# Routing of a hybrid mixer and mixture-of-experts block: both levels of the choice at once, the first selection on VectorE, rows normalised in pieces, and the first gather among the up matmuls

## The chip, the cores and the metric

The kernel runs on one core of one Trainium2 chip. The metric is the device time of one launch in microseconds (us), as the median of three runs.

## The reference

One layer over x of 256 tokens by 2048 channels, in fp32. What matters here is its second half:

```python
def _hier_moe(h, w_rg, b_rg, w_re, b_re, w1, w3, w2):
    lg = (ht @ w_rg).astype(jnp.float32) + b_rg.astype(jnp.float32)
    pg = jax.nn.softmax(lg, axis=-1)
    p_top, g_idx = lax.top_k(pg, 1)
    le = jnp.einsum("td,dge->tge", ht, w_re).astype(jnp.float32) + b_re.astype(jnp.float32)
    le_sel = jnp.take_along_axis(le, ..., axis=1)[:, 0]
    l2, e_idx = lax.top_k(le_sel, TOPK_IN_GROUP)
    gate = jax.nn.softmax(l2, axis=-1) * p_top
    expert = g_idx * EXP_PER_GROUP + e_idx
    ...
        return (jax.nn.silu(xb @ w1[e]) * (xb @ w3[e])) @ w2[e]

x = x + (jax.nn.sigmoid(mix_a) * ya + jax.nn.sigmoid(mix_b) * yb) @ w_out
x = x + _hier_moe(_rmsnorm(x, norm_ffn), w_rg, b_rg, w_re, b_re, w1, w3, w2)
return _rmsnorm(x, norm_final)
```

There are 4 groups of 8 experts. Each token chooses one group and the two best experts in it. An expert has three weights of 4 MB each (2048 by 512), so all 32 have 402 MB. Ahead of this stand two mixers (a gated delta rule with 8 heads and gated linear attention with 4), whose projections take 120 chunks of weights of 1 MB.

## The kernel before

Each engine has one program, written out by hand in its order, and semaphores tie them together. The mixer stages and the output projection come first (until about 960 us). TensorE multiplies chunks of weights that ScalarE and VectorE have split into two parts (`chunk`, L1361 to L1363; L668; L931). While TensorE makes the last output columns, it also transposes x1 (L1644) and multiplies it with the router's weights (L1654), which gives the logits.

**Routing.** VectorE (L1222 to L1299) sums the squares, GpSimd makes the reciprocal root `rstd2` (L627, L628), and ScalarE scales x1 by it into `h2`, in two copies of 2048 columns, one for each half of the tokens (L871). VectorE adds the biases to the logits (L1246, L1247), finds the largest group, masks the experts to that group, and finds first and second in it. `link(...)` makes the next instruction wait until this one is finished. The result is `Mt`, the mask of tokens by 32 experts (L1273), and `Wt`, their weights (L1287). TensorE counts ranks over tokens with five products (L1682 to L1686). From them VectorE makes `pos`, the slot of a token in its expert (L1291), and the number of rounds of 64 tokens an expert needs (`rounds_ready`, L1299). Every engine reads that number into a register (`value_load`, in the program's order a TENSOR_LOAD). It is one round for these inputs.

**Experts.** Experts run in 16 pairs, with 64 token slots each. For each pair GpSimd compares `pos` with `iota` into the 0/1 matrix `sel` (L642, L646) and weights it into `selg` (L649). TensorE gathers the rows by a product of `h2` with `sel`, in four quarters (L1702), and VectorE multiplies each quarter by the norm's scale into `xeT` (L1308, semaphore `xe`). TensorE transposes `selg` (L1710), ScalarE copies it (L884). Then come the up matmuls for both experts, w1 and w3 in four quarters each (L1729), the activation (L889, L1315, L1318, transposed at L1738), the down matmuls (L1749), and the products that add the result into x1 (L1765, L1324). The gather of the next pair stands among the matmuls of the one before.

**Weights.** SyncE alone loads them (`load_pair`, L452), in transfers of 1 MB, into a ring of 16 slots, 24 to a pair. The first 16 go out as places come free from the stages before; the later ones wait for `slotM_free`, which each quarter of the up matmuls raises by two at its end, and each quarter of the down matmuls too.

## Time and profile before

| | |
|---|---|
| median of 3 runs | 1941.43 us (1941.38 to 1942.59) |
| the profiled execution | 1936.88 us |
| its span in the profile | 1935.1 us |
| mean granted TensorE clock | 0.977 |
| busy: TensorE, VectorE, ScalarE, GpSimd | 1796.2, 638.6, 431.1, 176.8 us |
| read from memory | 534.42 MB |

### The profile page before, as it was taken

The page shows a single profiled execution, that of the slowest core. Times are in us where ns is not written, and L with a number is a line of the kernel's source. Part 1 is how long each engine was busy: PE and PEld are TensorE (multiplying, and loading weights), DVE is VectorE, ACT ScalarE, POOL GpSimd, SP SyncE. Part 2 cuts the span into 40 slices and gives each one's busy share as a digit, 9 for nine tenths or more (in the row PEclk, how much of TensorE's full clock was granted, in tenths as well). Part 3 has the DMA queues.
Part 4 walks back from the last instruction along what each step waited for, and adds up shares of the span by engine and source line. Part 5 has one row for each costly group of instructions (what it writes and reads, how often), then busy time and mean ns, then how long its engine had stood idle before and what let it go on. Part 6 is the DMA issues. An engine that isn't in the chain of part 4 may idle for free.

```text
span 1935.1 us, 21374 instructions
## 1 busy us (share of the span) xinstructions
PE 1796.2 (93%) x8774; PEld 1117.1 (58%) x8774; DVE 638.6 (33%) x674; ACT 431.1 (22%) x443; POOL 176.8 (9%) x211
## 2 busy tenths in 40 slices
PE   5999998999898989999979999999999999999996
PEld 4777776787777878888744444443443434443342
DVE  3245756643473345564311110111110111101112
ACT  3344334422452233334310000000000000000001
POOL 4000013240114110000000000000000000000000
PEclk8999999999998999999989999999999999999999
DMA  6434433432343235665869999999999999999996
GB/s 183 151 127 156 132 129 122 153 117 82 115 152 110 66 91 176 195 215 177 339 260 421 421 422 421 422 421 422 422 422 421 422 422 422 422 422 422 421 421 271
DMA packets 120456, 537.36 MB, mean 278 GB/s; under 512 B 8700, under 2 KB 8764, under 8 KB 70348
## 3 DMA queue, kind: packets, MB, share of 16 engines
q1 hardware_dynamic: 119808, 535.86, 70.9%
q0 software_dynamic: 592, 0.69, 0.3%
q8 instruction: 43, 0.70, 0.2%
q14 instruction: 13, 0.11, 0.0%
HBM read 534.42 MB, written 2.10 MB: 277 GB/s over the span
## 4 chain that ended last, share of the span: by engine, by line
PE 73%; DMA 15%; DVE 6%; ACT 3%; issue 2%; POOL 1%; DVEq 0%; POOLq 0%; SPq 0%; ACTq 0%
PE psum L1729 18%; DMA arena<-in_w 14%; PE psum L1361 10%; PE psum L1362 10%; PE psum L1363 10%; PE psum L1749 6%; PE psum L1765 6%; PE psum L1702 5%; DVE w_lo L931 2%; ACT w_hi L668 1%; PE psum L1551 1%; PE psum L1554 1%; PE psum L1557 1%; DMA arena<-in_w_in 1%; PE psum L1394 1%
## 5 line engine op out<-in xcount | busy, mean ns | idle before, releaser
L1729 PE MATMUL psum<-arena 128*64 128x512 f32 x2048 | 445.4, 593 | 13.8 <-DMA arena<-in_w 13.1
L931 DVE TENSOR_TENSOR w_lo<-arena,w_hi 128x2048 fp32r<-128x2048 f32 x120 | 276.9, 2309 | 349.4 <-ACT w_hi L668 343.1
L1361 PE MATMUL psum<-w_hi,hT_hi 128*128 128x512 f32 x832 | 341.9, 411 | 35.2 <-DVE w_lo L931 21.0
L1362 PE MATMUL psum<-w_lo,hT_hi 128*128 128x512 f32 x832 | 335.6, 403 | 0.0
L1363 PE MATMUL psum<-w_hi,hT_lo 128*128 128x512 f32 x832 | 335.4, 403 | 0.0
L1729 PEld LDWEIGHTS psum<-arena 128*64 128x64 f32 x2048 | 144.3, 137 | 312.5 <-issue 283.7
L668 ACT ACTIVATE w_hi<-arena 128x2048 fp32r<-128x2048 f32 x120 | 229.3, 1913 | 314.1 <-PE psum L1363 308.4
L1749 PE MATMUL psum<-arena 128*64 128x512 f32 x1024 | 226.3, 595 | 15.6 <-DMA arena<-in_w 14.7
L1361 PEld LDWEIGHTS psum<-w_hi,hT_hi 128*128 128x128 f32 x832 | 161.0, 194 | 77.3 <-DVE w_lo L931 17.2
L1363 PEld LDWEIGHTS psum<-w_hi,hT_lo 128*128 128x128 f32 x832 | 160.3, 193 | 39.4
L1362 PEld LDWEIGHTS psum<-w_lo,hT_hi 128*128 128x128 f32 x832 | 161.2, 194 | 36.7
L1749 PEld LDWEIGHTS psum<-arena 128*64 128x64 f32 x1024 | 70.3, 137 | 159.5 <-issue 125.4
L1308 DVE TENSOR_TENSOR arena<-psum,arena 128x512 f32<-128x512 f32 x64 | 44.3, 692 | 315.9 <-PE psum L1702 315.9
L1702 PEld LDWEIGHTS psum<-arena 128*128 128x128 f32 x1024 | 119.4, 194 | 30.6 <-issue 24.3
L1702 PE MATMUL psum<-arena 128*128 128x128 f32 x1024 | 126.5, 280 | 6.1 <-POOL arena L646 6.1
L1765 PE MATMUL psum<-arena 128*128 128x512 f32 x256 | 112.6, 593 | 0.0
L1324 DVE TENSOR_TENSOR arena<-arena,psum 128x512 f32<-128x512 f32 x128 | 88.0, 687 | 42.0 <-PE psum L1765 42.0
L889 ACT ACTIVATE arena<-psum 128x512 f32<-128x512 f32 x16 | 9.6, 597 | 373.1 <-PE psum L1729 373.1
L899 ACT ACTIVATE arena<-psum 128x512 f32<-128x512 f32 x64 | 38.2, 597 | 228.7 <-PE psum L1749 228.7
L642 POOL TENSOR_TENSOR arena<-arena 128x128 f32<-128x128 f32 x32 | 12.1, 401 | 794.2 <-PE psum L1702 773.3
L1315 DVE SCALAR_TENSOR_TENSOR arena<-arena,psum 128x512 f32<-128x512 f32 x16 | 11.0, 687 | 222.3 <-ACT arena L889 222.3
L1318 DVE TENSOR_TENSOR arena<-arena,psum 128x512 f32<-128x512 f32 x16 | 11.0, 687 | 214.3 <-PE psum L1729 214.3
(324 smaller groups left out, 1242.6 us busy)
## 6 DMA issues: line engine op xcount, KB each, us to landing
arena<-in_w SPq DMA_DIRECT2D x384, 1024.0 KB, 26.2
arena<-in_w_in SPq DMA_DIRECT2D x88, 1024.0 KB, 5.0
arena<-in_w_out SPq DMA_DIRECT2D x16, 1024.0 KB, 5.1
arena<-in_w_oa SPq DMA_DIRECT2D x8, 1024.0 KB, 5.0
arena<-in_w_ob SPq DMA_DIRECT2D x8, 1024.0 KB, 5.1
arena<-in_x SPq DMA_DIRECT2D x4, 1024.0 KB, 7.8
out_y<-arena SPq DMA_DIRECT2D x2, 1024.0 KB, 4.0
arena<-in_norm_final SPq DMA_DIRECT2D x1, 1024.0 KB, 18.6
```

Of the source, the lines that this page charges most:

```text
L668: nc.scalar.activation(w_hi[x % NSPLIT], ringA[:, x % RING_A, :], ACT.Copy).then_inc(sem("w_hi"), 1)
L899: nc.scalar.activation(Ysb[:, k * CB:(k + 1) * CB], bank(4 + k), ACT.Copy).then_inc(sem("yev"), 1)
L931: tt(w_lo[x % NSPLIT], ringA[:, x % RING_A, :], w_hi[x % NSPLIT].bitcast(F32), ALU.subtract)\
L1308: tt(xeT[u][:, 4 * b:4 * b + 4, :], bank(2 + b % 2).rearrange("p (k s) -> p k s", k=4), nffn[:, 4 * b:4 * b + 4].unsqueeze(2).to_broadcast ...
L1324: tt(x1[:, m, k * CB:(k + 1) * CB], x1[:, m, k * CB:(k + 1) * CB], bank(4 + (2 * k + m) % 4), ALU.add).then_inc(sem("xadd"), 1)
L1361: mm(m_banks[m], lhs[0][:, k0 + k, ms], wh[:, cs], start=(start and k == 0), stop=False)
L1362: mm(m_banks[m], lhs[0][:, k0 + k, ms], wl[:, cs], start=False, stop=False)
L1363: i = mm(m_banks[m], lhs[1][:, k0 + k, ms], wh[:, cs], start=False, stop=(stop and k == CT - 1))
L1702: i = mm(bank(2 + b % 2)[:, k * P:(k + 1) * P], h2[:, m, 4 * b + k, :], sel[:, m * P:(m + 1) * P], start=(m == 0), stop=(m == NM - 1))
L1729: i = mm(bank(w)[e * CAP:(e + 1) * CAP, :], xeT[u][:, CT * q + k, e * CAP:(e + 1) * CAP], src[e][:, k * CB:(k + 1) * CB], start=(q == 0 an ...
L1749: i = mm(bank(4 + k)[e * CAP:(e + 1) * CAP, :], aT[:, t * P + e * CAP:t * P + (e + 1) * CAP], src[e][:, k * CB:(k + 1) * CB], start=(t == ...
L1765: mm(bank(4 + j % 4), comb[u][:, m * P:(m + 1) * P], Ysb[:, k * CB:(k + 1) * CB], start=True, stop=True).then_inc(sem("cmb"), 1)
```

## The change

It does seven things.
- VectorE finds first and second in all four groups at once, on 64 columns, and masks to the chosen group at the end. The running counts restart in each group through `restart_g` and `restart_e`. Several independent instructions share one `link`.
- VectorE itself makes the first pair's `sel` and `selg` (semaphores `sel0`, `selg0`), right behind `pos`, and the number of rounds after them. `iota` counts from 1, so `pos` isn't lowered by 1. GpSimd begins with the second pair, and takes the slots used off `pos` pair by pair.
- The ranks are given free after three products; the two of the count go to bank 4.
- ScalarE makes `h2` in four quarters, with the two exponentials of the routing behind the second.
- TensorE gathers two quarters before the first up matmuls and the other two ahead of their second and third quarter, and transposes `selg` between w1 and w3.
- The first two pairs are written out. TensorE reads the number of rounds between them. SyncE issues the loads of the first two pairs (32 transfers) ahead of its read.
- In the mixer stages some pairs of semaphores become one (`kbg` and `kdec`, `eg` and `ekd`, the steps of the softplus).

The core of the diff:

```diff
@@ -461,10 +460,10 @@
             wait(sp, ("ss2", 1))
             wait(sp, ("logits", NC))
             load_pair(0, 0, 0, RING_M - 1, RING_M, first=True)
+            load_pair(0, 0, 0, RING_M, PER_PAIR)
+            load_pair(1, 0, 1, 0, PER_PAIR)
             wait(sp, ("rounds_ready", 1))
             rounds = sp.value_load(rounds_i[0:1, 0:1], min_val=1, max_val=SEQ // CAP)
-            load_pair(0, 0, 0, RING_M, PER_PAIR)
-            load_pair(1, 0, 1, 0, PER_PAIR)
             with sp.Fori(1, rounds * (PAIRS // UNROLL)) as i:
                 with sp.Fori(i & (PAIRS // UNROLL - 1), (i & (PAIRS // UNROLL - 1)) + 1) as p:
                     for u in range(UNROLL):
...
-            with pool.Fori(0, rounds) as r:
-                with pool.Fori(0, PAIRS) as p:
-                    n = r * PAIRS + p
...
+                i.then_inc(sem("selg"), 1)
+                for m in range(NM):
+                    col = pos[:, bass.ds(m * NE + 2 * p, 2)]
+                    nc.gpsimd.tensor_tensor(col, col, iota[:, CAP - 1:CAP].to_broadcast([P, 2]), ALU.subtract)
                 pool.drain()
+
+            with pool.Fori(1, rounds * PAIRS) as n:
+                with pool.Fori(n & (PAIRS - 1), (n & (PAIRS - 1)) + 1) as p:
+                    select(n, p)
...
             wait(act, ("rstd2", 1))
-            for m in range(NM):
-                nc.scalar.activation(h2[:, m], x1[:, m, :].rearrange("p (c k) -> p k c", k=KT), ACT.Copy,
-                                     scale=rstd2[:, m:m + 1]).then_inc(sem("h2"), 1)
+            def h2_piece(b):
+
+                for m in range(NM):
+                    nc.scalar.activation(h2[:, m, 4 * b:4 * b + 4, :],
+                                         x1[:, m, :].rearrange("p (c k) -> p k c", k=KT)[:, 4 * b:4 * b + 4, :],
+                                         ACT.Copy, scale=rstd2[:, m:m + 1]).then_inc(sem("h2"), 1)
+
+            h2_piece(0)
+            h2_piece(1)
             wait(act, ("r_d", 1))
-            nc.scalar.activation(rt["ed"], rt["d"], ACT.Exp).then_inc(sem("r_ed"), 1)
+            nc.scalar.activation(rt["ed"], rt["d"], ACT.Exp).then_inc(sem("r_exp"), 1)
             wait(act, ("r_dm", 1))
-            nc.scalar.activation(rt["e2"], rt["dm"], ACT.Exp).then_inc(sem("r_e2"), 1)
+            nc.scalar.activation(rt["e2"], rt["dm"], ACT.Exp).then_inc(sem("r_exp"), 1)
+            h2_piece(2)
+            h2_piece(3)

             wait(act, ("rounds_ready", 1))
             more_rounds = act.value_load(rounds_i[0:1, 1:2], min_val=0, max_val=SEQ // CAP - 1)
...
+            nc.vector.memset(rt["restart_g"], 1.0)
+            link(nc.vector.memset(rt["restart_e"], 1.0))
+            nc.vector.memset(rt["restart_g"].rearrange("p (m g) -> p m g", m=NM)[:, :, 0:1], 0.0)
+            link(nc.vector.memset(rt["restart_e"].rearrange("p (s e) -> p s e", e=EPG)[:, :, 0:1], 0.0))
             dve.wait_ge(sem("sq2"), NM * NC)
             nc.vector.reduce_sum(ss2, ssp.rearrange("p (m c) -> p m c", m=NM), axis=AX.X).then_inc(sem("ss2"), 1)
...
             for m in range(NM):
+                i = stt(m_(rt["l"])[:, m, :], lp[m], rstd2[:, m:m + 1], bias, ALU.mult, ALU.add)
             link(i)
...
+            nc.vector.reduce_max(rt["gm"], lg, axis=AX.X)
+            link(nc.vector.tensor_reduce(m_(rt["m1"]), le, AX.X, ALU.max))
+            gm = rt["gm"].unsqueeze(2).to_broadcast([P, NM, GROUPS])
+            tt(m_(rt["d"]), lg, gm, ALU.subtract).then_inc(sem("r_d"), 1)
+            tt(m_(rt["eqg"]), lg, gm, ALU.is_equal)
+            link(tt(mge(rt["eq1"]), le, over_e(rt["m1"]), ALU.is_equal))
+            scan(rt["cumg"], rt["restart_g"], rt["eqg"], 0.0, ALU.mult, ALU.add)
+            link(scan(rt["cum1"], rt["restart_e"], rt["eq1"], 0.0, ALU.mult, ALU.add))
+            stt(rt["fg"], rt["cumg"], 1.0, rt["eqg"], ALU.is_le, ALU.mult)
+            link(stt(rt["f1"], rt["cum1"], 1.0, rt["eq1"], ALU.is_le, ALU.mult))
+            link(stt(mge(rt["ls2"]), mge(rt["f1"]), NEG, le, ALU.mult, ALU.add))
+            link(nc.vector.tensor_reduce(m_(rt["m2"]), mge(rt["ls2"]), AX.X, ALU.max))
             tt(rt["dm"], rt["m2"], rt["m1"], ALU.subtract).then_inc(sem("r_dm"), 1)
+            link(tt(mge(rt["eq2"]), mge(rt["ls2"]), over_e(rt["m2"]), ALU.is_equal))
+            link(scan(rt["cum2"], rt["restart_e"], rt["eq2"], 0.0, ALU.mult, ALU.add))
+            link(stt(rt["f2"], rt["cum2"], 1.0, rt["eq2"], ALU.is_le, ALU.mult))
+            link(tt(rt["ls2"], rt["f1"], rt["f2"], ALU.add))
+            tt(mge(Mt), mge(rt["ls2"]), over_e(rt["fg"]), ALU.mult).then_inc(sem("Mt"), 1)
+
+            dve.wait_ge(sem("r_exp"), 1)
+            nc.vector.reduce_sum(rt["den"], m_(rt["ed"]), axis=AX.X)
+            dve.wait_ge(sem("r_exp"), 2)
             link(ts(rt["s2"], rt["e2"], 1.0, None, ALU.add))
+            link(tt(m_(rt["s2"]), m_(rt["s2"]), rt["den"].unsqueeze(2).to_broadcast([P, NM, GROUPS]), ALU.mult))
             link(nc.vector.reciprocal(rt["r2"], rt["s2"]))
+            link(stt(rt["w1"], rt["r2"], 0.5, rt["fg"], ALU.mult, ALU.mult))

             dve.wait_ge(sem("ranks"), 1)
             dve.wait_ge(sem("Mt"), 1)
             link(tt(pos, bank(1, NM * NE), Mt, ALU.mult))
-            link(ts(pos, pos, 1.0, None, ALU.subtract))
-            link(nc.vector.reduce_max(rt["mx"], bank(2, NE), axis=AX.X))
+            pm, wm = m_(pos)[:, :, 0:2], m_(Wt)[:, :, 0:2]
+
+            def slots(t):
+                return t.unsqueeze(3).to_broadcast([P, NM, 2, CAP])
+
+            tt(sel.rearrange("p (m e s) -> p m e s", m=NM, e=2),
+               iota.unsqueeze(1).unsqueeze(1).to_broadcast([P, NM, 2, CAP]), slots(pm), ALU.is_equal)\
+                .then_inc(sem("sel0"), 1)
+            link(tt(rt["w2"], rt["w1"], rt["e2"], ALU.mult))
+            tt(mge(rt["wa"]), mge(rt["f1"]), over_e(rt["w1"]), ALU.mult)
+            link(tt(mge(rt["f2"]), mge(rt["f2"]), over_e(rt["w2"]), ALU.mult))
+            link(tt(Wt, rt["wa"], rt["f2"], ALU.add))
+            dve.wait_ge(sem("sel0"), 1)
+            tt(selg.rearrange("p (m e s) -> p m e s", m=NM, e=2), sel.rearrange("p (m e s) -> p m e s", m=NM, e=2),
+               slots(wm), ALU.mult).then_inc(sem("selg0"), 1)
+            ts(pm, pm, float(-CAP), None, ALU.add)
+
+            dve.wait_ge(sem("ranks"), 2)
+            link(nc.vector.reduce_max(rt["mx"], bank(4, NE), axis=AX.X))
...
-            mm(bank(1)[:, NE:2 * NE], ones, Mt[:, 0:NE], start=False, stop=True)
-            mm(bank(2, NE), ones, Mt[:, 0:NE], start=True, stop=False)
-            mm(bank(2, NE), ones, Mt[:, NE:2 * NE], start=False, stop=True).then_inc(sem("ranks"), 1)
-            wait(pe, ("rounds_ready", 1))
-            wait(pe, ("h2", 2))
+            mm(bank(1)[:, NE:2 * NE], ones, Mt[:, 0:NE], start=False, stop=True).then_inc(sem("ranks"), 1)
+            mm(bank(4, NE), ones, Mt[:, 0:NE], start=True, stop=False)
+            mm(bank(4, NE), ones, Mt[:, NE:2 * NE], start=False, stop=True).then_inc(sem("ranks"), 1)

             pe.sem_inc(sem("slotM_free"), RING_M)
             pe.sem_inc(sem("gath"), 4)
             pe.sem_inc(sem("combT"), 1)
             pe.sem_inc(sem("xadd"), 8)
-            more_rounds = pe.value_load(rounds_i[0:1, 1:2], min_val=0, max_val=SEQ // CAP - 1)

             def gather(n, b, first=False):

+                if first:
+                    pe.wait_ge(sem("h2"), 2 * (b + 1))
                 if not first or b >= 2:
                     pe.wait_ge(sem("xe"), n * 4 + (b - 1))
                 for k in range(4):
@@ -1705,12 +1718,15 @@

             def weights_in(n):

-                pe.wait_ge(sem("selg"), n + 1)
+                if isinstance(n, int) and n == 0:
+                    wait(pe, ("selg0", 1))
+                else:
+                    pe.wait_ge(sem("selg"), n)
                 for m in range(NM):
                     i = tr(bank(1)[:, m * P:(m + 1) * P], selg[:, m * P:(m + 1) * P], ident)
                 i.then_inc(sem("combT"), 1)

-            def expert_pair(n, it, u, more):
...
-                pe.wait_ge(sem("xe"), n * 4 + 4)
+                if not first:
+                    pe.wait_ge(sem("xe"), n * 4 + 4)
                 for w in range(2):
                     if w:
+                        if first:
+                            weights_in(n)
                         pe.wait_ge(sem("comb"), n + 1)
                     for q in range(4):
+                        if first and w == 0:
+                            pe.wait_ge(sem("xe"), q + 1)
+                            if q in (1, 2):
+                                gather(n, q + 1, first=True)
                         src = arrived(8 * w + 2 * q)
                         for k in range(CT):
                             for e in range(2):
@@ -1731,7 +1754,7 @@
                                        stop=(q == 3 and k == CT - 1))
                         i.then_inc(sem("slotM_free"), 2)
                 if more:
-                    pe.wait_ge(sem("sel"), n + 2)
+                    pe.wait_ge(sem("sel"), n + 1)
                     gather(n + 1, 0)
                 pe.wait_ge(sem("hid"), n + 1)
                 for t in range(FT):
@@ -1765,14 +1788,17 @@
                         mm(bank(4 + j % 4), comb[u][:, m * P:(m + 1) * P], Ysb[:, k * CB:(k + 1) * CB], start=True,
                            stop=True).then_inc(sem("cmb"), 1)

-            pe.wait_ge(sem("sel"), 1)
-            for b in range(4):
+            wait(pe, ("sel0", 1))
+            for b in range(2):
                 gather(0, b, first=True)
-            weights_in(0)
-            with pe.Fori(0, more_rounds * (PAIRS // UNROLL) + (PAIRS // UNROLL - 1)) as i:
+            expert_pair(0, 0, 0, True, first=True)
+            wait(pe, ("rounds_ready", 1))
+            more_rounds = pe.value_load(rounds_i[0:1, 1:2], min_val=0, max_val=SEQ // CAP - 1)
+            expert_pair(1, 0, 1, True)
+            end = more_rounds * (PAIRS // UNROLL) + (PAIRS // UNROLL - 1)
+            with pe.Fori(1, end) as i:
                 for u in range(UNROLL):
                     expert_pair(i * UNROLL + u, i, u, True)
-            end = more_rounds * (PAIRS // UNROLL) + (PAIRS // UNROLL - 1)
             expert_pair(more_rounds * PAIRS + (PAIRS - 2), end, 0, True)
             expert_pair(more_rounds * PAIRS + (PAIRS - 1), end, 1, False)
```

The orders of three engines show it. On TensorE, from the ranks to the first up matmuls, before:

```order
L1682 MATMUL psum<-arena 128x32 [waits Mt]
...
L1694 TENSOR_LOAD rounds_i [waits rounds_ready,h2]
L1702 MATMUL psum<-arena 128x128 [waits sel]
L1702 MATMUL psum<-arena 128x128 x15
L1702 MATMUL psum<-arena 128x128 [waits xe]
L1702 MATMUL psum<-arena 128x128 x7
L1702 MATMUL psum<-arena 128x128 [waits xe]
L1702 MATMUL psum<-arena 128x128 x7
L1710 MATMUL psum<-arena 128x128 [waits selg]
L1729 MATMUL psum<-arena 64x512 [waits slotM0]
```

And now:

```order
L1696 MATMUL psum<-arena 128x32 [waits Mt]
...
L1715 MATMUL psum<-arena 128x128 [waits h2,sel0]
L1715 MATMUL psum<-arena 128x128 [waits h2]
L1752 MATMUL psum<-arena 64x512 [waits slotM0,xe]
L1715 MATMUL psum<-arena 128x128 [waits xe,h2]
L1752 MATMUL psum<-arena 64x512 [waits slotM1]
L1715 MATMUL psum<-arena 128x128 [waits xe,h2]
L1752 MATMUL psum<-arena 64x512 [waits slotM2]
L1752 MATMUL psum<-arena 64x512 [waits slotM3,xe]
L1726 MATMUL psum<-arena 128x128 [waits selg0]
L1752 MATMUL psum<-arena 64x512 [waits slotM4,comb]
```

Each named product is the first of eight. The read of `rounds_i` has left this place, and two of the four gathers and the transposes stand behind the first up matmuls. On VectorE, behind the ranks, before:

```order
L1291 TENSOR_TENSOR arena<-psum,arena 128x64 [waits Mt,ranks]
L1292 TENSOR_SCALAR arena<-arena 128x64 [waits dve_link]
L1293 TENSOR_REDUCE arena<-psum 128x1 [waits dve_link]
...
L1299 TENSOR_TENSOR rounds_i<-arena 128x1
L1302 TENSOR_LOAD rounds_i [waits rounds_ready]
L1308 TENSOR_TENSOR arena<-psum,arena 128x512 [waits gath] x4
```

And now:

```order
L1289 TENSOR_TENSOR arena<-psum,arena 128x64 [waits Mt,ranks,dve_link]
L1295 TENSOR_TENSOR arena<-arena 128x256 [waits dve_link]
...
L1303 TENSOR_TENSOR arena<-arena 128x256 [waits sel0,dve_link]
L1305 TENSOR_SCALAR arena<-arena 128x2x2
L1308 TENSOR_REDUCE arena<-psum 128x1 [waits ranks]
...
L1314 TENSOR_TENSOR rounds_i<-arena 128x1
L1317 TENSOR_LOAD rounds_i [waits rounds_ready]
L1323 TENSOR_TENSOR arena<-psum,arena 128x512 [waits gath] x4
```

L1295 and L1303 are the first selection; the count and the register read still stand ahead of the four multiplications of gathered rows. On SyncE, before:

```order
L452 DMA arena<-in_w 128x2048 [waits logits,ss2]
L465 TENSOR_LOAD rounds_i [waits rounds_ready]
L465 ISA x2
L452 DMA arena<-in_w 128x2048 [waits slotM_free] x32
L468 UNCONDITIONAL_BRANCH
```

And now:

```order
L451 DMA arena<-in_w 128x2048 [waits logits,ss2]
L451 DMA arena<-in_w 128x2048 [waits slotM_free] x32
L466 TENSOR_LOAD rounds_i [waits rounds_ready]
L466 ISA x2
L467 UNCONDITIONAL_BRANCH
```

The read has moved behind 32 loads.

## Rows read from the trace of the kernel before

**Rows 1.** The page's DMA issues: count, KB each, median us to landing.
```profile
arena<-in_w SPq DMA_DIRECT2D x384, 1024.0 KB, 26.2
```

**Rows 2.** Windows: length, busy PE, PEld, DVE, ACT, POOL, then PEclk, DMA share, GB/s.
```profile
940.00:960.00 20.00, 20.00 (x99) 16.29 (x97) 5.05 (x3) 6.08 (x7) 0.00 (x0) 1.00 1.01 421
976.00:978.00 2.00, 0.00 (x0) 0.00 (x0) 0.00 (x0) 0.00 (x0) 0.76 (x2) 0.50 0.09 33
982.00:983.00 1.00, 1.00 (x7) 1.00 (x7) 0.00 (x0) 0.00 (x0) 0.00 (x0) 0.50 0.00 0
983.00:984.00 1.00, 1.00 (x11) 1.00 (x11) 0.59 (x1) 0.00 (x0) 0.00 (x0) 0.99 0.00 0
994.00:996.00 2.00, 2.00 (x12) 0.68 (x10) 0.00 (x0) 0.00 (x0) 0.00 (x0) 1.00 0.85 254
1100.00:1900.00 800.00, 773.32 (x3761) 326.23 (x3761) 129.62 (x189) 51.34 (x93) 28.77 (x61) 1.00 1.01 422
```

**Rows 3.** Chain of waits, pieces in order of time: start us, us, what.
```profile
989.60 27.69 PE psum L1729 x128
...
1046.28 27.62 PE psum L1729 x128
...
1382.25 6.87 PE psum L1765 x16
...
1441.98 6.87 PE psum L1765 x16
```

**Rows 4.** Timeline near the end: start us, us, engine, line, operation.
```profile
1912.39 3.65 PE L1749 MATMUL psum<-arena 128*64 128x512 f32 x16 [1.32 <-DMA arena<-in_w]
```

**Rows 5.** Timeline of the first pair: SyncE's first issue, gathers, combine products.
```profile
993.29 74.83 SPq L452 DMA_DIRECT2D arena<-in_w  x36
...
1035.57 3.84 PE L1702 MATMUL psum<-arena 128*128 128x128 f32 x32
...
1039.24 7.03 PE L1765 MATMUL psum<-arena 128*128 128x512 f32 x16
```

**Rows 6.** Timeline from the reciprocal root to the first pair.
```profile
964.23 7.38 ACT L871 ACTIVATE arena<-arena 128x2048 f32<-128x2048 f32 x2 [0.41 <-POOL arena L628]
966.02 0.22 DVE L1246 SCALAR_TENSOR_TENSOR arena<-psum,arena 128x4 f32<-128x4 f32 x1 [2.91 <-PE psum L1654]
...
969.90 0.16 DVE L1268 TENSOR_TENSOR arena<-arena 128x2 f32<-128x2 f32 x1
969.98 0.17 DVE L1269 TENSOR_TENSOR arena<-arena 128x16 f32<-128x16 f32 x1
970.18 0.18 DVE L1270 TENSOR_SCALAR arena<-arena 128x16 f32<-128x16 f32 x1
970.39 0.25 DVE L1238 TENSOR_TENSOR_SCAN arena<-arena 128x8 f32<-128x8 f32 x2
...
971.10 0.22 DVE L1273 TENSOR_TENSOR arena<-arena 128x64 f32<-128x64 f32 x1
971.38 0.64 PE L1682 MATMUL psum<-arena 128*128 128x32 f32 x2 [5.46 <-DVE arena L1273]
...
973.11 0.61 PE L1686 MATMUL psum<-arena 128*128 128x32 f32 x2
...
975.05 0.15 DVE L1299 TENSOR_TENSOR rounds_i<-arena 128x1 int32<-128x1 f32 x1
976.70 0.76 POOL L642 TENSOR_TENSOR arena<-arena 128x128 f32<-128x128 f32 x2 [12.50 <-issue]
...
979.80 8.93 PE L1702 MATMUL psum<-arena 128*128 128x128 f32 x64 [6.08 <-POOL arena L646]
...
983.41 0.69 DVE L1308 TENSOR_TENSOR arena<-psum,arena 128x512 f32<-128x512 f32 x1 [8.21 <-PE psum L1702]
...
988.57 0.38 PE L1710 MATMUL psum<-arena 128*128 128x128 f32 x2
```

**Rows 7.** Groups by form on VectorE: count, busy us, mean ns, idle before.
```profile
L1260 DVE TENSOR_REDUCE arena<-arena 128x16 f32<-128x64 f32 x1 | 0.3, 266 | 0.0
L1259 DVE TENSOR_TENSOR arena<-arena 128x64 f32<-128x64 f32 x1 | 0.2, 226 | 0.0
```

116 lines of the change are left out of this document (39 added, 77 removed), and 7 rows, old and new, of the table rt.

## The prediction

> **What bounds the kernel now.** I read the page first, then the windows, then the chain of waits. The page lists 384 weight transfers of 1 MB, one per ring slot, with a median of 26.2 us from issue to landing [rows 1]: they stand in a queue. The windows show why [rows 2]: from 1100 to 1900 us all transfer engines are busy at 422 GB/s, while TensorE is busy 773 of 800 us. The chain of waits shows the same limit as a period [rows 3]. The first pair of experts starts at 989.60 and the second at 1046.28, so TensorE alone needs 56.6 to 56.7 us for a pair (27.69 of it up matmuls). Late in the stage the second piece of successive pairs comes at 1382.25 and 1441.98, 59.7 us apart. That is the transfers' pace: 24 slots in 59.7 us is 2.49 us for a slot. So in the expert stage TensorE is faster than the weights. TensorE's last wait for a weight ends at 1912.39 [rows 4], and the end follows it with a tail that the change leaves alone.
>
> The transfers are continuous except for one hole. They run at 421 GB/s in 940 to 960, have fallen to 33 GB/s in 976 to 978, and are back inside the window from 994 to 996 [rows 2]. 254 of 422 GB/s there is 1.2 of 2 us, so the restart is at 994.8. From there 368 slots and the load of the final norm's scale, another 1 MB, make 369 x 59.7/24 = 917.9 us, which ends at 1912.7, where the last wait ends too: the end of the kernel is the restart plus a constant. In the hole all 16 slots are full, and SyncE's next load waits for the first up matmuls to free two: they start at 989.60, 3.45 us is a quarter of one weight (27.69/8), and the issue row stands at 993.29 [rows 5]. The bytes follow 1.75 us behind the release (993.05 to 994.8). **So a microsecond of earlier first release is a microsecond of the kernel, as long as later releases keep up.**
>
> **What lies before that release** [rows 6]: VectorE routes from 966.02 to Mt at 971.10, TensorE makes ranks from 971.38, VectorE makes the count of rounds until 975.20, GpSimd reads it and begins the selection 1.50 us later (976.70), TensorE gathers from 979.80 to 988.57 in four quarters, transposes the weights, and starts the first up matmuls.
>
> **The change, part by part.** (1) The chain to Mt. Behind the logits the new VectorE order has 19 instructions, 7 of them issued with no wait behind another one. Their durations I take from the nearest shapes [rows 7]: 0.23 us for 64 elements, 0.27 for a reduction, 0.17 for 8, and 0.25 for the scan of 64, which no row shows (two scans of 8 take 0.25 together, so one is no slower than its neighbours). A waited step costs its duration plus 0.03 us (970.18 to 970.39 for one of 0.18), an unwaited one its duration less 0.08 to 0.09 (969.90 to 969.98 for one of 0.16) [rows 6]. The sum puts Mt at 969.71 instead of 971.10: 1.4 us earlier. The four memsets go into VectorE's wait for ScalarE's squares, and cost nothing.
>
> The Trainium skill says in "VectorE: DVE Perf Modes", section "The DRAIN you can't avoid", that leaving out the semaphore between VectorE instructions saves nothing. By that rule the 7 unwaited steps would each cost about 0.11 us more, and the time would be 0.8 us above mine. This trace has the 0.08 us spacing in its rows, so here the row decides, for small instructions at least.
>
> (2) Selection. TensorE starts ranks at 970.0. They take 2.3 us to the end of the fifth product (971.38 to 973.11, plus 0.61), so 972.3. VectorE can start pos after the third (971.5) and needs 0.26 for it and about 0.43 for the comparison over 256 elements (between 0.23 for 64 and 0.69 for 512 [rows 6, 7]), so 972.2. GpSimd, its register read and the round count drop out of the way: the first gather starts at 972.35 instead of 979.80, 7.45 us earlier. ScalarE makes the normalised rows: two 2048-wide copies took 7.38 us from 964.23 [rows 6], so four 512-wide ones take about 3.8 and the first two quarters are there at 968.1, the exponentials by 969, the third quarter at 971, the fourth at 973. All are ahead of their users.
>
> (3) The clock. TensorE's granted clock stood at the lower level from 976 until 983 [rows 2], and the first gather took 3.6 us (979.80 to VectorE's start at 983.41), while two at the full clock take 3.67 from start to the next work, 1.84 each [rows 5]. I keep 3.6 for the first gather and 1.8 for the second, since TensorE is idle before ranks here too. Now only two gathers stand ahead of the first up matmuls: 972.35 + 3.6 + 1.8 = **977.75 instead of 989.60, 11.85 us earlier**. If the clock came back during ranks it would be 1.8 us earlier still.
>
> (4) What the first pair takes on. Two gathers (3.7) and the transposed weights with ScalarE's copy (at most the 1.03 from 988.57 to 989.60 [rows 3, 6]; I take 1.0) now stand between its up matmuls: 4.7 us. Counted from the start T of the up matmuls, releases come at T+3.45, 8.7, 14.0 and 17.5, and the transfers of two slots take 4.97, so they idle twice for 0.3 us. The second pair starts at T+56.6+4.7 = T+61.3, releases at T+64.75, and bytes can follow at T+66.5; the transfers, undisturbed, would have wanted that slot at T+64.9, which the kernel before could give (T+61.8). This costs 1.6 us, the 0.6 of the small stalls included. From there TensorE gains 3.1 us a pair on the transfers and is never late again.
>
> (5) The register read. TensorE's read of the round count moves from a time when it was waiting for GpSimd anyway to the seam between pair 0 and 1. Below nothing it cannot cost; no row shows it alone. GpSimd's, with its branches, took 1.50 [rows 6], and TensorE's own had ended when the gather began, 4.6 us after the count was ready. The nearest row is the 1.50, and 7.0 us of queued combine matmuls [rows 5] stand ahead of it that may cover it, so I take half, 0.75, and keep 0 and 4.6 for the range. It falls on the slot that is already late, so it counts in full. VectorE's read sits ahead of its first multiplication of gathered rows: count ready at 974.4, read 1.5, multiplication 0.69, so 976.6, which is 1.1 us ahead of TensorE's need. SyncE's read follows 32 loads and hides between releases 3.45 us apart.
>
> The Trainium skill ("Advanced Engine Details and Errata", section "Sequencer Loop") says that other engine instructions can be read and queued while a control instruction executes. With that the read at the seam would cost nothing, and the time would be 0.75 us below mine. No run here shows it yet.
>
> (6) The merged semaphores of the mixer stages move a wait by one small instruction beside full TensorE work, and GpSimd's extra subtraction follows its selection, behind which it idles for most of a pair: nothing.
>
> **Sum.** 11.85 earlier, less 1.6, less 0.75 = 9.5 us. The profiled execution took 1936.88 us (span 1935.1), so it would be 1927.4; the median of the runs is 1941.43, 4.55 above the profiled one, and I carry the same difference: **1931.9 us**.
>
> **Rivals.** (a) A register read is long. VectorE's read is bounded only by its 8.2 us between 975.20 and 983.41. At that bound the first up matmuls start at 983.4 and 5.6 us are lost; with TensorE's at 4.6 in place of 0.75 another 3.9. The first alone gives 1937.5, both 1941.4, no change. For it: no row shows either read. Against: GpSimd's 1.50. Chance 0.07. (b) TensorE sets the end. If each pair kept TensorE's pace, the gain would be 11.85 - 4.7 - 0.75 = 6.4 us, 1935.0. Against it stands the period of 59.7 against 56.6. Chance 0.05. (c) The change does not do what it says: TensorE starts early but something late still holds the first release, the fourth quarter of rows or the weights' copy. Then the start is between mine and the old one, some 1937; the orders of the engines show no such wait. Chance 0.03. (d) Slower: code. Pair 0 and pair 1 are now written out beside the loop, so TensorE's instructions for them come from memory once more, while the transfer engines are saturated. A fetch that queues like a weight takes 26.2 us [rows 1]; one such stall in pair 0 costs 26.2 less the 9.5 gained: 1958. It decides from 13.4 us of stall on (slower by 0.2%). Against: from 940 to 960 TensorE ran 20.00 of 20.00 us on written-out code with the transfers at 421 GB/s [rows 2]. Chance 0.03.
>
> **How the numbers follow.** My case has 0.82. Its own range: the start of the up matmuls from 976.0 (clock back) to 980.3 (waited steps throughout, second gather slow too), the seam from 0 to 1.5: 1929.4 to 1935.2. I widen it to 1928.8 to 1936.4, which takes in (b) and leaves out (a), (c) partly, and (d). A change of 0.2% is 3.9 us, about what a measurement can tell from no change. My case, (b) and the better half of (a) and (c) are faster by more: 0.92. Same 0.05, slower 0.03.
>
> **What would show it.** The first up matmuls near 978 instead of 989.6; a gap of transfers of some 6.5 us instead of 18.5; two short dips and one near the second pair's start; then 422 GB/s to the end; the last weight's wait ending 9 to 10 us before 1912.4; the late period still 59.7. Wrong would be: a TensorE gap at the seam above 2 us, VectorE's first multiplication later than 978, TensorE idle within pair 0 without a transfer or semaphore behind it, or a changed period.

## The result and the profile after

The changed kernel took 1928.93 us (median of 6 runs, 1927.68 to 1931.47) against 1938.67 for the kernel before on the same chips (6 runs, 1935.51 to 1942.59). The ratio is 0.9948, with a 95% interval of 0.9936 to 0.9960. The medians lie 9.7 us apart; by the ratio it is 10.1 us less, between 7.8 and 12.4. Its profiled execution took 1927.68 us, with a span of 1925.9.

The timeline of the changed kernel from the routing to the first up matmuls (start us, us, engine, line, operation, and in brackets idle time and what ended it), which answers to [rows 6]:

```profile
963.46 4.30 ACT L875 ACTIVATE arena<-arena 128x512 f32<-128x512 f32 x4 [0.47 <-POOL arena L627]
965.18 0.42 DVE L1258 SCALAR_TENSOR_TENSOR arena<-psum,arena 128x36 f32<-128x36 f32 x2 [2.84 <-PE psum L1668]
...
965.95 0.17 DVE L1263 TENSOR_TENSOR arena<-arena 128x8 f32<-128x8 f32 x1
966.04 0.16 DVE L1264 TENSOR_TENSOR arena<-arena 128x8 f32<-128x8 f32 x1
...
966.46 0.28 DVE L1267 TENSOR_TENSOR_SCAN arena<-arena 128x64 f32<-128x64 f32 x1
...
968.80 0.22 DVE L1277 TENSOR_TENSOR arena<-arena 128x64 f32<-128x64 f32 x1
...
969.08 0.64 PE L1696 MATMUL psum<-arena 128*128 128x32 f32 x2 [4.00 <-DVE arena L1277]
...
970.66 0.23 DVE L1289 TENSOR_TENSOR arena<-psum,arena 128x64 f32<-128x64 f32 x1 [0.85 <-PE psum L1698]
...
970.92 0.42 DVE L1295 TENSOR_TENSOR arena<-arena 128x256 f32<-128x256 f32 x1
...
971.40 5.69 PE L1715 MATMUL psum<-arena 128*128 128x128 f32 x32
...
973.33 0.15 DVE L1314 TENSOR_TENSOR rounds_i<-arena 128x1 int32<-128x1 f32 x1
975.22 0.69 DVE L1323 TENSOR_TENSOR arena<-psum,arena 128x512 f32<-128x512 f32 x1 [1.74 <-PE psum L1715]
977.02 3.65 PE L1752 MATMUL psum<-arena 128*64 128x512 f32 x16
```

This execution reached the routing 0.84 us earlier than the one of before (965.18 against 966.02), so lengths from there are what to compare. Mt comes 3.62 us behind it (5.08 before), the first gather 6.22 (13.78), the first up matmuls 11.84 (23.58).

The same kernel's windows (length, busy PE, PEld, DVE, ACT, POOL, then PEclk, DMA share, GB/s), which answer to [rows 2]:

```profile
974.00:976.00 2.00, 2.00 (x14) 2.00 (x14) 0.69 (x1) 0.00 (x0) 0.00 (x0) 0.67 0.55 229
976.00:978.00 2.00, 2.00 (x16) 1.31 (x17) 0.69 (x1) 0.00 (x0) 0.00 (x0) 1.00 0.02 8
...
980.00:982.00 2.00, 2.00 (x16) 1.39 (x13) 0.00 (x0) 0.00 (x0) 0.00 (x0) 1.00 0.26 45
982.00:984.00 2.00, 2.00 (x14) 1.02 (x15) 0.69 (x1) 0.00 (x0) 0.00 (x0) 1.00 0.86 344
984.00:986.00 2.00, 2.00 (x12) 0.51 (x8) 0.00 (x0) 0.00 (x0) 0.00 (x0) 1.00 1.01 426
986.00:988.00 2.00, 2.00 (x18) 1.83 (x16) 0.00 (x0) 0.00 (x0) 0.00 (x0) 1.00 0.95 295
...
992.00:994.00 2.00, 2.00 (x12) 0.72 (x10) 0.00 (x0) 0.00 (x0) 0.00 (x0) 1.00 0.95 295
...
1042.00:1044.00 2.00, 2.00 (x12) 0.72 (x10) 0.00 (x0) 0.00 (x0) 0.00 (x0) 1.00 0.84 279
1044.00:1046.00 2.00, 2.00 (x12) 0.70 (x10) 0.00 (x0) 0.00 (x0) 0.00 (x0) 1.00 0.86 340
```

The transfers end in the window from 974 and are back at 982.2 (45 and 344 GB/s are 1.8 us at 422, counted back from 984). The hole is 7 us instead of 19. Behind it stand three dips: (422 - 295)/422 of 2 us is 0.6, twice, and 0.7 + 0.4 at 1042 to 1046, together 2.3 us.

The first pair and its seam, in the same kernel's timeline, with the last wait for a weight, which answer to [rows 5] and [rows 4]:

```profile
995.17 0.44 PE L1726 MATMUL psum<-arena 128*128 128x128 f32 x2
995.65 0.38 ACT L894 ACTIVATE arena<-psum 128x256 f32<-128x256 f32 x1 [23.43 <-PE psum L1726]
...
996.08 13.95 PE L1752 MATMUL psum<-arena 128*64 128x512 f32 x64 [0.47 <-ACT arena L894]
...
1009.97 2.05 PE L1715 MATMUL psum<-arena 128*128 128x128 f32 x16
...
1031.99 7.03 PE L1788 MATMUL psum<-arena 128*128 128x512 f32 x16
...
1038.95 2.37 PE L1752 MATMUL psum<-arena 128*64 128x512 f32 x10
...
1903.18 3.65 PE L1772 MATMUL psum<-arena 128*64 128x512 f32 x16 [1.31 <-DMA arena<-in_w]
```

From the last up matmul of pair 0 to the second pair's first, 1009.97 to 1038.95, pass 28.98 us, as before (1017.22 to 1046.20). TensorE's register read lies in there and costs nothing. The up matmuls with what is put between them take 32.95 us (27.62 before). The late period is unchanged: in the chain of waits the combine products (L1788) of successive pairs stand 59.7 us apart, as before [rows 3].

```profile
1491.34 6.87 PE psum L1788 x16
...
1551.01 6.87 PE psum L1788 x16
```

### The profile page after: what moved, and what is told of

Read it like the earlier page. It is cut to its first block, busy times and chain, and to the rows that moved or that the text cites. A ratio compares the mean times of both kernels' runs of the same rounds, so it can differ in the third digit from the quotient of the medians.

```text
span 1925.9 us, 21447 instructions
## 1 busy us (share of the span) xinstructions
PE 1798.1 (93%) x8774; PEld 1117.9 (58%) x8774; DVE 637.9 (33%) x670; ACT 432.0 (22%) x449; POOL 178.4 (9%) x235
## 4 chain that ended last, share of the span: by engine, by line
PE 75%; DMA 13%; DVE 6%; ACT 3%; issue 2%; POOL 1%; SPq 0%; DVEq 0%; POOLq 0%; ACTq 0%
PE psum L1752 19%; DMA arena<-in_w 12%; PE psum L1376 10%; PE psum L1377 10%; PE psum L1378 10%; PE psum L1772 7%; PE psum L1788 6%; PE psum L1715 5%; DVE w_lo L941 2%; PE psum L1566 1%; ACT w_hi L670 1%; PE psum L1569 1%; PE psum L1572 1%; DMA arena<-in_w_in 1%; PE psum L1409 1%
## 5 line engine op out<-in xcount | busy, mean ns | idle before, releaser
L1788 PE MATMUL psum<-arena 128*128 128x512 f32 x256 | 112.6, 593 | 0.0
```

The costliest lines, as they stand in the source:

```text
L1788: mm(bank(4 + j % 4), comb[u][:, m * P:(m + 1) * P], Ysb[:, k * CB:(k + 1) * CB], start=True, stop=True).then_inc(sem("cmb"), 1)
```

## The experiments

Since launches differ ahead of the routing, two lengths are read in each profile: from VectorE's first routing instruction to the first up matmuls ("start"), and from it to TensorE's last wait for a weight ("stage"). The last column runs from the second pair's first up matmul to that last wait. All are in us, and each row is one profiled execution.

| kernel | start | stage | second pair to last wait |
|---|---|---|---|
| before, first profile | 23.58 | 946.37 | 866.19 |
| before, repeated | 23.57 | 945.97 | 865.79 |
| mixer_only | 23.58 | 945.96 | 865.78 |
| changed, first profile | 11.84 | 938.00 | 864.23 |
| changed, repeated | 11.85 | 937.73 | 863.96 |
| gather_first | 15.26 | 939.20 | 867.34 |
| delay_first | 18.98 | 944.71 | 863.81 |
| quarter_first | 10.78 | 941.34 | 863.94 |
| pool_select | 14.86 | 940.94 | 864.15 |
| all_links | 12.32 | 938.47 | 864.21 |
| warm | 10.99 | 936.97 | 864.05 |
| best | 10.97 | 936.59 | 864.23 |
| best2 | 9.71 | 935.09 | 863.98 |

### The kernel before, repeated

No edit.

> The kernel before, run and profiled once more, to learn how far its own executions lie apart. The median given with the prediction was 1941.43 us, a later group of three runs lay near 1935.6, and the profiled one took 1936.88. Theory 1 (the launches of this kernel differ by up to 7 us from group to group, whatever its code, in the mixer stages ahead of the routing): the time where VectorE begins the routing moves against 966.02 us by as much as the span does, and the expert stage keeps its 946.4 us from there to TensorE's last wait for a weight (1912.39). Theory 2 (the difference lies in the weight transfers of the expert stage): the 946.4 moves, the 966.02 does not. Between 1935 and 1943 us.

It took 1937.16 us (10 runs, 1935.98 to 1942.55). The kernel it was compared with, the same one, took 1934.76 to 1943.20 in 26 runs on that chip: 16 lie up to 1938.22, 10 from 1941.06 on, none between. On the two chips of the later runs some lie between as well (1938.94, 1939.12, 1940.66, 1940.71, 1940.87), and one of those 22 launches took 5873.40 us; the ratios leave it out. The stage moved by 0.4 us and the start by 0.01. The routing began at 966.45. What tells theory 1 from theory 2 came with another run: gather_first's profiled execution reached the routing at 971.64. That is 5.2 and 5.6 us later than in the two profiles of the kernel before, and 6.5 and 6.7 later than in those of the changed kernel, whose code is the same up to there. Its windows beside those of the kernel before show one place where it happens. In gather_first:

```profile
490.00:500.00 10.00, 8.19 (x48) 7.44 (x47) 3.58 (x2) 3.81 (x5) 0.00 (x0) 0.83 0.43 135
...
530.00:540.00 10.00, 10.00 (x43) 8.52 (x42) 3.75 (x5) 2.11 (x4) 0.00 (x0) 0.81 0.00 0
```

In the kernel before:

```profile
490.00:500.00 10.00, 8.19 (x64) 7.50 (x63) 3.99 (x4) 4.43 (x5) 0.00 (x0) 1.00 0.64 200
...
530.00:540.00 10.00, 10.00 (x45) 8.03 (x44) 6.06 (x8) 1.91 (x1) 0.00 (x0) 1.00 0.00 0
```

A share of 0.8 says that the clock stood at the lower level for part of the window. VectorE's split of chunk 56 (493 us) was 1.6 us late and that of chunk 60 (537 us) 3.9. This fits theory 1: what differs between launches lies in the mixer stages, and the clock has a part in it. In the 26 runs the mean granted clock says the same, 0.972 in all 10 of the upper group and 0.976 or 0.977 in the 16 of the lower. But no launch of the upper group was profiled, so where those lose their 5 us is not shown.

### The changed kernel, repeated

No edit.

> The changed kernel once more. Its profile had the routing's start at 965.18 (0.84 earlier than before) and the last wait for a weight 938.0 us behind it, 8.4 less than before, where the sum of the prediction had 9.5. Theory 1 (both the 0.84 and the missing 1.1 are spread between executions): this profile gives another start, within 1 us of 966, and a stage length between 936.5 and 938. Theory 2 (the merged semaphores of the mixer stages are worth the 0.84): the start is 965.2 again and differs from that of the kernel before in its repeated run by 0.8. Ratio to the kernel before 0.995, between 0.9935 and 0.9965.

It took 1928.72 us (6 runs, 1926.41 to 1932.66), ratio 0.9948 (0.9929 to 0.9968). The start is the same to 0.01 us, the stage 0.27 shorter, the routing begins at 964.90, a little outside the expected 1 us around 966. The lead at that point was 0.84 us and is 1.55 in the repeated pair, so it varies. Two profiles of each kernel don't tell whether the changed kernel owns part of it; theory 2's cause for it falls with the next run. The stage's gain, 8.0 to 8.6 us, is short of 9.5 in every pairing: that much of theory 1 falls.

### The merged semaphores alone

```diff
-                pe.wait_ge(sem("kbg"), g + 1)
-                pe.wait_ge(sem("kdec"), g + 1)
+                pe.wait_ge(sem("k_scaled"), g + 1)
...
-            nc.scalar.activation(eg, gcol, ACT.Exp).then_inc(sem("eg"), 1)
-            nc.scalar.activation(ekd, gdif, ACT.Exp).then_inc(sem("ekd"), 1)
+            nc.scalar.activation(eg, gcol, ACT.Exp)
+            nc.scalar.activation(ekd, gdif, ACT.Exp).then_inc(sem("eg"), 1)
```

> The kernel before with the merged semaphores of the mixer stages alone. Theory 1 (nothing hangs on them): ratio 1.000, within 0.1%, the routing's start equal to that of the repeated kernel before within 0.3 us. Theory 2 (they gave the 0.84 us): start 0.8 us earlier.

Ratio 0.9996 (0.9982 to 1.0009), routing at 967.30, later than either profile of the kernel before. They are worth nothing that can be seen.

### All gathers first

```diff
-                        if first:
-                            weights_in(n)
...
-                            if q in (1, 2):
-                                gather(n, q + 1, first=True)
...
-            for b in range(2):
+            for b in range(4):
                 gather(0, b, first=True)
+            weights_in(0)
```

> The changed kernel with all four gathers of the first pair and the transposed weights ahead of its first up matmuls, as before. Theory (the restart of the transfers sets the end, and part of an earlier restart is given back by later releases): up matmuls start 4.7 us later (981.7 by the clock of the first profile), the transfers restart 4.7 us later, but without the three dips, 2.3 us in all, so the time is 2.4 us above the changed kernel and 7 below the kernel before (ratio 0.9963). Rival A (the dips don't count): 4.7 us above. Rival B (the dips give everything back): no difference.

It took 1932.22 us (9 runs), ratio 0.9961 (0.9946 to 0.9977), where 0.9963 was expected. In its profile the start is 15.26, 3.4 later and not 4.7:

```profile
986.59 0.38 PE L1726 MATMUL psum<-arena 128*128 128x128 f32 x2
...
986.79 0.69 DVE L1323 TENSOR_TENSOR arena<-psum,arena 128x512 f32<-128x512 f32 x1 [1.09 <-PE psum L1715]
...
986.90 27.69 PE L1748 MATMUL psum<-arena 128*64 128x512 f32 x128
```

The first up matmuls follow 0.31 us behind the transposes (1.03 before), since each quarter of them now waits only for its own gathered rows: the last multiplication still runs until 987.48, and ScalarE's copy begins at 987.01. And counted from the routing's start the clock came back some 0.8 us earlier than in the changed kernel (9.4 us behind it, at 981.0, against 10.1), which made the gathers 0.4 us shorter. The transfers show no dip. The stage is 1.2 us longer than the changed kernel's first profile and 1.5 longer than its second, less than half of the 3.4 by which the start is later: rival A falls, and so does B by 1.3 us. The intervals of the two ratios overlap, so only the stage tells them apart.

### A delay ahead of the first up matmuls

```diff
+            def idle_products(count):
+                for _ in range(count):
+                    mm(bank(0)[:, 0:P], ident, ident, start=True, stop=True)
...
+            idle_products(32)
             expert_pair(0, 0, 0, True, first=True)
```

> The changed kernel with 32 products of 128x128 that nobody needs between the second gather and the first up matmuls of pair 0 (0.235 us each, 7.5 us). The stage from VectorE's first routing instruction to TensorE's last wait for a weight has 937.9 us in the changed kernel (two profiles: 938.0 and 937.7). Theory (the first releases set the end): the stage grows by the whole 7.5, to 945.4 within 0.5. Rival (the transfers have slack that takes it up): it grows by less than half of that.

The start grew by 7.1 us and the stage by 6.8: one for one, to 0.3. The products took 7.3 us and not 7.5, so the stage, 944.71, is just short of the expected 945.4 within 0.5. The rival falls.

### Slower pairs

```diff
+                if more and not first:
+                    idle_products(10)
```

> The changed kernel with 10 such products at the end of each pair from the second to the fifteenth, 2.35 us each and 33 in all. Theory (transfers bound the stage: 59.7 us a pair against TensorE's 56.6): TensorE's pair goes to 59.0, still under 59.7, and the stage stays at 937.9 within 0.7. Rival (TensorE sets the end): 33 us more, 971.

The chain of waits of this kernel:

```profile
1038.40 27.62 PE psum L1757 x128
...
1097.24 27.62 PE psum L1757 x128
...
1862.07 27.64 PE psum L1757 x128
```

The second pair took 58.84 us instead of 56.6. 14 such pairs end at 1862.07, and the span is 962.3 us from the routing's start against 960.7 and 960.5: 1.7 us more for the 31.5 us that were added. That is outside the expected 0.7 and far from the rival's 33. Transfers bound the stage of the changed kernel. Here TensorE's slack, some 30 us by these numbers, is used up: from the second pair on it waits for no weight, not for the last one either, so this kernel has no place in the table.

### GpSimd selects for the first pair

```diff
-            tt(sel.rearrange("p (m e s) -> p m e s", m=NM, e=2),
-               iota.unsqueeze(1).unsqueeze(1).to_broadcast([P, NM, 2, CAP]), slots(pm), ALU.is_equal)\
-                .then_inc(sem("sel0"), 1)
...
+            wait(pool, ("pos0", 1))
+            for m in range(NM):
+                nc.gpsimd.tensor_tensor(
+                    s4[:, m], io, pos[:, m * NE:m * NE + 2].unsqueeze(2).to_broadcast([P, 2, CAP]), ALU.subtract)
+            pool.drain()
+            nc.gpsimd.tensor_scalar(sel, sel, 0.0, None, ALU.is_equal).then_inc(sem("sel0"), 1)
```

> The changed kernel with GpSimd making the first pair's selection, as soon as VectorE has pos, and no longer behind the count of rounds. Theory (VectorE's selection is worth what GpSimd's instructions take more): GpSimd needed 3.05 us from its first instruction to the end of the comparison, VectorE 0.42, so the first gather starts 2.6 us later and the stage takes 940.5. If the pause of 1.42 us between GpSimd's two instructions was only its first time in the loop, 1.3 us later and 939.2.

Its timeline:

```profile
971.76 0.22 DVE L1305 TENSOR_TENSOR arena<-psum,arena 128x64 f32<-128x64 f32 x1 [0.85 <-PE psum L1707]
...
972.06 0.76 POOL L656 TENSOR_TENSOR arena<-arena 128x128 f32<-128x128 f32 x2 [7.54 <-DVE arena L1305]
...
974.23 0.87 POOL L659 TENSOR_SCALAR arena<-arena 128x256 f32<-128x256 f32 x1 [1.41 <-issue]
975.16 6.05 PE L1724 MATMUL psum<-arena 128*128 128x128 f32 x32 [2.64 <-POOL arena L659]
```

The start is 3.0 us later and the stage 3.1 longer. The pause of 1.41 us is there outside a loop too. The loop's own first selection has none:

```profile
999.94 0.76 POOL L638 TENSOR_TENSOR arena<-arena 128x128 f32<-128x128 f32 x2 [23.69 <-PE psum L1735]
1000.86 0.85 POOL L642 TENSOR_SCALAR arena<-arena 128x256 f32<-128x256 f32 x1 [0.16 <-issue]
```

In the changed kernel the same loop's first selection, the first that GpSimd makes there, has 1.42. So the pause belongs to GpSimd's first selection, wherever that stands. VectorE's selection is worth 3 us to the start: the first gather comes 2.66 later without it (2.6 expected), and the two gathers take 0.36 longer, since the clock comes back later in them. Of the 7.56 us by which the changed kernel's first gather is earlier than in the kernel before, the other 4.9 are Mt's 1.46 and no longer standing behind the count of rounds and GpSimd's register read.

### One quarter first

```diff
+                            if q:
+                                gather(n, q, first=True)
                             pe.wait_ge(sem("xe"), q + 1)
-                            if q in (1, 2):
-                                gather(n, q + 1, first=True)
...
-            for b in range(2):
-                gather(0, b, first=True)
+            gather(0, 0, first=True)
```

> The changed kernel with one gather ahead of the first up matmuls, and each of the others right ahead of the quarter that uses it. The up matmuls start earlier (one gather less, 1.87 us, but a wait of 0.8 for VectorE's multiplication: 1.0 earlier), and pair 0 gets longer (one gather more inside, 1.98, and three waits of 0.8: 4.4). Theory (it is the second pair's first release that sets the end now, since the transfers already dip there): the second pair starts 3.3 us later and the stage takes 3.3 us more, 941.2. Rival (the very first release sets the end): 1.0 less, 936.9.

The up matmuls start 1.06 us earlier, the second pair (1045.48, 77.4 us behind the routing's start against 73.8) 3.6 later, and the stage is 3.5 us longer. The first release came earlier and the kernel ended later: in the changed kernel it is the second pair's start that counts. The table's last column says it in nine profiles of eight kernels: from that start to the last wait pass 863.8 to 864.2 us. In the four profiles with all gathers ahead of the first up matmuls the second pair is not late, and the length is 865.8 to 867.3.

### Waits everywhere

```diff
-            tt(m_(rt["eqg"]), lg, gm, ALU.is_equal)
+            link(tt(m_(rt["eqg"]), lg, gm, ALU.is_equal))
...
-            scan(rt["cumg"], rt["restart_g"], rt["eqg"], 0.0, ALU.mult, ALU.add)
+            link(scan(rt["cumg"], rt["restart_g"], rt["eqg"], 0.0, ALU.mult, ALU.add))
```

> The changed kernel with a wait behind every instruction on VectorE's way to Mt (7 more). Theory (an unwaited step saves about 0.11 us): Mt 3.62 + 0.8 = 4.4 us behind the first routing instruction, up matmuls 12.6 behind it instead of 11.84, stage 938.7. Rival (waits on the same engine cost nothing): 3.6, 11.8 and 937.9.

Mt came at 972.04, 4.50 us behind 967.54 (3.62 without the waits): 0.88 us for 7 waits, 0.13 each. The start moved by 0.48 only, since the clock came back earlier in its gathers (3.1 us behind their start against 3.9), and the stage by 0.6. The rival falls. The Trainium skill's "VectorE: DVE Perf Modes", section "The DRAIN you can't avoid", has it that a wait between VectorE instructions costs nothing; for instructions of 0.16 to 0.29 us these runs show 0.13 us.

### TensorE kept busy

```diff
+            idle_products(5)
             transpose_x1(NC - 1)
+            idle_products(5)
             route(NC - 1)
+            idle_products(14)
```

> The changed kernel with products that nobody needs in TensorE's three waits of the routing (5, 5 and 14 of them), so that it is hardly idle before ranks. Theory 1 (the lower clock behind the idle time costs 1.9 us in the gathers and 0.7 in ranks; then VectorE's count of rounds and register read, ready by 974.5, become the limit): granted clock 1.0 through ranks and both gathers, the two gathers 3.7 us instead of 5.6, up matmuls 11.84 - 1.8 = 10.0 us behind VectorE's first routing instruction, stage 936.1. Theory 2 (the extra products delay ranks, or the clock falls anyway): 11.8 or more and no gain.

It took 1927.81 us, ratio 0.9943 (0.9925 to 0.9960). The clock stayed up through ranks and fell in the first gather:

```profile
968.00:970.00 2.00, 2.00 (x20) 2.00 (x20) 1.79 (x13) 2.00 (x3) 0.00 (x0) 1.00 1.02 422
970.00:972.00 2.00, 1.19 (x12) 1.00 (x10) 1.79 (x10) 2.00 (x5) 0.00 (x0) 1.00 1.02 426
...
974.00:976.00 2.00, 2.00 (x14) 2.00 (x14) 1.33 (x10) 0.88 (x1) 0.00 (x0) 0.64 1.02 426
```

0.85 us of start were gained, 0.63 of them in ranks and 0.22 in the two gathers (5.40 us against 5.62), where theory 1 put 0.7 and 1.9. It was right for ranks only.

### Count of rounds later, another bank

```diff
-                    i = tr(bank(1)[:, m * P:(m + 1) * P], selg[:, m * P:(m + 1) * P], ident)
+                    i = tr(bank(5 if isinstance(n, int) and n == 0 else 1)[:, m * P:(m + 1) * P],
+                           selg[:, m * P:(m + 1) * P], ident)
...
+            gathered(0, 0, range(2))
+            dve.wait_ge(sem("ranks"), 2)
...
+            gathered(0, 0, range(2, 4))
```

> As the one with products in the waits, and besides: VectorE multiplies the first two gathered quarters before it counts the rounds and reads the register, and the first pair's transposed weights go through bank 5, so that the w3 matmuls don't wait for ScalarE's copy. Theory: up matmuls 9.2 us behind the first routing instruction (2.65 less than the changed kernel), 0.45 less inside pair 0, stage 934.8, ratio to the kernel before 0.993. If VectorE's read was not the limit, this one and the one before start their up matmuls alike.

It took 1927.34 us, ratio 0.9943 (0.9927 to 0.9958). The start equals warm's (10.97), so VectorE's read was not the limit. Pair 0 took 61.39 us instead of 61.93, the 0.5 of the bank, and the stage is 0.4 shorter than warm's.

### No gap in TensorE's work

```diff
+            idle_products(17)
...
-            mm(bank(4, NE), ones, Mt[:, 0:NE], start=True, stop=False)
-            mm(bank(4, NE), ones, Mt[:, NE:2 * NE], start=False, stop=True).then_inc(sem("ranks"), 1)
+            idle_products(4)
```

There are 17 products where best has 14. The two products of ranks stand behind the second gather.

> As best, but TensorE's waits are filled more closely: 17 products instead of 14 behind the logits, and 4 wide ones in place of the last two products of ranks, which move behind the second gather (only the count of rounds needs them). In best the clock still fell at about 972, inside the first gather, behind a stretch in which TensorE was busy 1.2 of 2 us, and the up matmuls started 10.97 us behind the first routing instruction, the stage took 936.6. Theory (that stretch is what lets the clock fall): granted clock 1.0 from 960 to 977, the two gathers 3.7 us, up matmuls 9.2 to 9.5 us behind, stage 935.0. Rival (it falls whatever the products, or the moment drifts from launch to launch): 10.9 and 936.6.

```profile
970.00:972.00 2.00, 1.88 (x17) 1.69 (x15) 1.61 (x10) 2.00 (x3) 0.00 (x0) 1.00 1.02 426
972.00:974.00 2.00, 2.00 (x19) 1.95 (x19) 1.18 (x7) 1.61 (x2) 0.00 (x0) 1.00 1.02 426
974.00:976.00 2.00, 2.00 (x22) 2.00 (x20) 0.75 (x2) 0.00 (x0) 0.00 (x0) 1.00 1.02 414
```

The clock stands at the upper level throughout, the two gathers take 3.7 us, the start is 9.71 and the stage 935.09, where 935.0 was expected. It took 1926.77 us (6 runs, 1925.11 to 1928.34), ratio 0.9937 (0.9921 to 0.9953). By the stage it is 2.8 us shorter than the changed kernel. The intervals of the two ratios overlap, so the runs alone don't show that.

## Why the prediction was right, and where it was wrong

**What bounds the stage** was right. A delay ahead of the first up matmuls came out at the end (7.1 in, 6.8 out), and 31.5 us spread over later pairs cost 1.7.

**The start of the up matmuls** was right: 11.74 us earlier, against 11.85. Mt gave 1.46 (1.4 expected), the first gather came 7.56 earlier (7.45), the clock rose inside the gathers (5.62 us until the up matmuls; I had 5.4).

**The loss in the first pair** was right in sum and wrong in its parts. Inside it 5.3 us were added, not 4.7: a gather put between up matmuls costs 1.98 with its seam instead of 1.84, and each quarter standing alone 0.13 more. The copy took 0.9. TensorE's register read cost 0, not 0.75. By the rule of the Trainium skill's "Advanced Engine Details and Errata", section "Sequencer Loop", it would cost nothing, and the trace agrees. Pair 0 took 61.93 us, against 62.05. The dips sum to 2.3 us, against 2.35, but the two in the first pair are 0.6 each where I had 0.3, and the one at the second pair's start is 1.1 where I had 1.75 with the register read. That the sums agree is luck: a gather dearer than expected and a read that cost nothing cancel.

**The expert stage's end** was about 1.2 us worse than summed (0.9 to 1.5 by the pairing of profiles): the gain in the stage is 8.0 to 8.6, not 9.5. Even gather_first, with no dip, took 923.9 us from its first up matmul to its last wait, and the kernel before 922.4 to 922.8. Both move 387.2 MB by their windows. In the kernel before the bytes last until 1912.9 (188 GB/s in the window from 1912), 0.5 us behind the last wait:

```profile
1912.00:1914.00 2.00, 1.61 (x8) 0.63 (x10) 0.00 (x0) 0.48 (x1) 0.00 (x0) 1.00 0.45 188
```

In the changed one the bytes left at 1900 (385, 176 and 16 GB/s in three windows of 2 us) are worth 2.7 us, and the last wait ends at 1903.18, 0.45 behind that:

```profile
1900.00:1902.00 2.00, 1.87 (x10) 0.42 (x6) 0.00 (x0) 0.00 (x0) 0.00 (x0) 1.00 0.93 385
1902.00:1904.00 2.00, 0.82 (x4) 0.34 (x6) 0.00 (x0) 0.00 (x0) 0.00 (x0) 1.00 0.42 176
1904.00:1906.00 2.00, 2.00 (x12) 0.72 (x10) 0.00 (x0) 1.19 (x2) 0.00 (x0) 1.00 0.04 16
```

So the last weight comes at the frayed end and no longer half a microsecond ahead of the last bytes, which makes 0.95 of the difference. gather_first ends in the same way (352, 139 and 16 GB/s from 1908, the last wait at 1910.84, 0.4 behind), so the order of the gathers is not what does it. Why the last weight changes its place stays open.

**The time in microseconds** is where the prediction went wrong, and the step is the last one of its sum. It took 1941.43 as the base and carried the 4.55 us between that median and the profiled execution. Measured, the changed kernel's median lies 1.25 us above its profiled execution and that of the kernel before 1.8 above its own (1938.67), so 3.3 us too much were carried, and 1931.9 came out as 1928.93. The three runs behind it, 1941.38 to 1942.59, all fell into the upper of two groups. In 26 further runs 16 lie in the lower one. The first three runs of the changed kernel, measured with them, have a median of 1928.66, just under my low end of 1928.8, and all six 1928.93, just over it. Counted from the profiled execution, with no difference carried, the sum gave 1927.4 for an execution that took 1927.68. That closeness is luck in part: the stage gave 1.1 less, and the execution reached the routing 0.84 earlier. I had read a profile 4.5 us under its own runs and treated that as a constant; it differs from launch to launch, by all signs with the clock in the mixer stages, and a range had to hold it. As a ratio the forecast was 0.9951, against 0.9948, and that is luck in part too. The stage accounts for 8.3 us. What the medians show beyond it lies ahead of the routing. On one chip the changed kernel's repeated runs (1928.72) lie 7.8 us below the lower group of the kernel before (median 1936.5), which is the stage's gain; the upper group lifts that kernel's median above it. None of the changed kernel's 12 launches lies apart like that group (the highest is 1932.66). Whether the change has a hand in it is not shown.

**The rivals.** (a) fell: VectorE's multiplication began at 975.22, when the gather ended. (b) fell with the delay and the slower pairs. (c) fell: no wait stood in the way. (d) fell: four more packets of instructions were fetched (47 against 43 on the page), and TensorE shows no gap in the first two pairs but the 0.47 us for ScalarE's copy.

**Not run alone** were ScalarE's rows in quarters, the earlier release of ranks, and SyncE's 32 loads ahead of its register read. What each is worth stays open.

## What to carry to other kernels

Where a stage is bound by a ring of transfers, find the release that the stream waits for first, and then the one that is late next. Here the start of the second pair took over from the first release, and every microsecond put into the first pair counted from there, even one that made the first release earlier. Compare lengths from an anchor inside the profile when the part ahead of it varies more than the change is worth, and look at how single runs lie before taking a median of three as a base.
